# The last output projection of a two-layer backbone: from feature-major tiles to token-major pieces

## The reference

```
for i in range(DEPTH):
    need_ctx = i < DEPTH - 1
    ...
    h_lat = h_lat + g_l * (o_lat @ w_out[i])
    if need_ctx:
        h_ctx = h_ctx + g_c * (o_ctx @ w_out[i])
return h_lat
```

## Time and profile before

| what | value |
|---|---|
| median of 3 runs | 1484.33 us (1481.15, 1484.33, 1485.0) |
| the profiled execution: its time, its span | 1482.72 us, 1480.9 us |
| mean granted TensorE clock (1.0 is 2.4 GHz) | 0.992 |
| PE busy, VectorE busy, ScalarE busy | 97%, 67%, 37% of the span |
| first projection without its first tile, 841.0 to 1002.4 us | 161.4 us |
| norm stage, 1002.4 to 1040.4 us | 38.0 us |
| store of `hT` (L885): issued, landed after; SP's next weight load | 1005.9 us, 9.7 us; 1023.7 us |
| last projection, 1380.4 to 1475.6 us, and what follows it | 95.2 us, 5.3 us |

### The profile page before, as it was taken

The page is one execution under the profiler, slowest core; times in us unless marked ns, Lnnn a source line. Parts: engine busy times, 40 slices in busy tenths (PEclk is TensorE's granted clock), DMA queues, the critical chain, the costliest instruction groups (busy, mean ns, idle before and its releaser), DMA issues.

```text
span 1480.9 us, 18435 instructions
## 1 busy us (share of the span) xinstructions
PE 1434.7 (97%) x7415; PEld 1144.5 (77%) x7415; DVE 986.2 (67%) x1196; ACT 541.1 (37%) x764; POOL 237.3 (16%) x272
## 2 busy tenths in 40 slices
PE   5989999999999999999999899998999899999998
PEld 1336878888887878778888688888888778788998
DVE  3384998889988877786786554547455766555543
ACT  2554222221221433443323411216256455455432
POOL 1000333323332000000002043342000110000000
PEclk9999999999999999999999999999999999999999
DMA  9999555565555554454555766544334432323563
GB/s 344 400 360 347 193 176 169 156 227 156 185 168 150 193 185 135 132 170 175 164 209 203 257 216 230 200 152 132 114 114 143 142 114 90 110 87 113 191 221 129
DMA packets 65172, 272.23 MB, mean 184 GB/s; under 512 B 6784, under 2 KB 17216, under 8 KB 45376
## 3 DMA queue, kind: packets, MB, share of 16 engines
q1 hardware_dynamic: 44912, 193.45, 37.1%
q0 software_dynamic: 20176, 77.61, 16.2%
HBM read 256.36 MB, written 14.68 MB: 183 GB/s over the span
## 4 chain that ended last, share of the span: by engine, by line
PE 90%; DMA 4%; DVE 3%; ACT 1%; issue 1%; SPq 0%; ACTq 0%; POOL 0%; DVEq 0%
PE banks L1036 20%; PE banks L1037 20%; PE banks L1040 20%; DMA ada_ring<-in_ada_first 3%; PE banks L1984 2%; PE banks L1985 2%; PE banks L1990 2%; PE banks L1218 2%; PE banks L2147 2%; PE banks L1205 2%; PE banks L2019 1%; PE banks L1301 1%; PE banks L551 1%; PE banks L2118 1%; PE banks L2134 1%; PE banks L1269 1%
## 5 line engine op out<-in xcount | busy, mean ns | idle before, releaser
L1036 PE MATMUL banks<-xh,wh 128*128 128x512 f32 (+1 forms) x1536 | 538.3, 363 | 0.1
L1037 PE MATMUL banks<-xl,wh 128*128 128x512 f32 (+1 forms) x1536 | 525.3, 355 | 0.0
L998 DVE TENSOR_TENSOR wl<-raw,wh 128x2048 fp32r<-128x2048 f32 (+1 forms) x125 | 283.7, 2270 | 96.4 <-ACT wh L992 96.3
L1036 PEld LDWEIGHTS banks<-xh,wh 128*128 128x128 f32 x1536 | 290.1, 189 | 49.6 <-issue 9.3
L992 ACT ACTIVATE wh<-raw 128x2048 fp32r<-128x2048 f32 (+1 forms) x125 | 236.5, 1892 | 242.1 <-PE banks L1040 171.3
L1037 PEld LDWEIGHTS banks<-xl,wh 128*128 128x128 f32 x1536 | 290.3, 189 | 43.3 <-issue 3.8
L1040 PE MATMUL banks<-xh,wl 128*128 128x512 f32 (+1 forms) x1536 | 311.0, 355 | 0.0
L1040 PEld LDWEIGHTS banks<-xh,wl 128*128 128x128 f32 x1536 | 256.9, 189 | 40.5
L386 DVE SCALAR_TENSOR_TENSOR ada_acc<-ada_w,cond,ada_acc 128x1024 f32<-128x1024 f32 x120 | 160.1, 1334 | 5.1 <-DMA ada_w<-in_ada_rest 2.9
L409 POOL DMA_DIRECT2D ada_w<-in_ada_rest x128 | 69.3, 542 | 556.4 <-DVE ada_acc L398 381.4
L398 DVE SCALAR_TENSOR_TENSOR ada_acc<-ada_w,cond,ada_acc 128x1024 f32<-128x1024 f32 x90 | 125.3, 1392 | 0.0
(11 more groups left out here) (329 smaller groups left out, 1704.7 us busy)
## 6 DMA issues: line engine op xcount, KB each, us to landing
ada_w<-in_ada_rest POOLq DMA_DIRECT2D x128, 512.0 KB, 4.1
raw<-in_ev_tiles SPq DMA_DIRECT2D x52, 1024.0 KB, 6.7
ada_ring<-in_ada_first SPq DMA_DIRECT2D x32, 1024.0 KB, 12.4
raw<-in_out_tiles SPq DMA_DIRECT2D x32, 1024.0 KB, 5.1
raw<-in_od_wide SPq DMA_DIRECT2D x16, 1024.0 KB, 4.9
raw<-in_od_gates SPq DMA_DIRECT2D x16, 1024.0 KB, 4.9
hT<-in_hT POOLq DMA_DIRECT2D x4, 1024.0 KB, 11.9
spectra<-kstage POOLq DMA_DIRECT2D x4, 1024.0 KB, 10.6
```

Source lines behind the costliest of these rows:

```text
L998: nc.vector.tensor_tensor(b.wl[:, t % 2, 0:width], b.raw[:, t % 2, 0:width], b.wh[:, t % 2, 0:width].bitcast(F32), ALU.subtract).then_inc( ...
L1036: nc.tensor.matmul(out, wh[:, k, :], b.xh[:, seg, k, :], start=(k == 0), stop=False)
L1037: nc.tensor.matmul(out, wh[:, k, :], b.xl[:, seg, k, :], start=False, stop=False)
```

## The change

The last projection is written anew (`last_block`) and done token-major: four pieces of 512 output columns, each of four weight tiles (512 rows of `w_out` by 512 columns, 1024 KB as before) for two halves r of 128 tokens. Per weight tile and half there are 12 matmuls of 512 columns, with `xh` or `xl` as the stationary operand. The weight rows are taken in the order in which the attention units end (`WIDE_ROWS`). A piece is finished by VectorE in two steps per half: product times a broadcast row of gates (`grow`), plus the residual in token order (`hrow`). SP stores each half by itself (256 KB).

What that needs is made earlier. The first projection turns each hT tile after the next product (`turn_residual`; the last one in the norm stage), ScalarE copies four tiles at a time (`copy_residual`, after the splits of i = 5, 9, 13 and at the end of the norm stage), SP stores 512 KB four times (`store_residual`), the last time in layer 1. The gate column block is turned in the norm stage by one more transpose, copied, stored as a row of 8 KB and loaded back broadcast to 128 partitions (1024 KB) at slot 32 of layer 1. The store of `hT` and the waits on it go. Semaphores are renamed or shared (`gains_in` is now `spread_in`; `odd_mx` and `odd_rden` are joined to layer 0's), and `out_block` serves the first projection alone; the parts of the diff that do only that are left out.

```diff
-    return {"ev_tiles": tiles(a["ev_w_in"][0]), "out_tiles": np.stack([tiles(w) for w in a["w_out"]]),
+    return {"ev_tiles": tiles(a["ev_w_in"][0]), "out_tiles": tiles(a["w_out"][0]),
+            "out_wide": np.concatenate([wide(a["w_out"][1][:, c:c + 512]) for c in range(0, D, 512)]),
...
+    b.otok_late = put("otok_late", "ADA", 0, [P, 2, 512])
+    b.gate_rows = put("gate_rows", "ADA", 4 * K, [KT, P])
+    b.hrow = [put(f"hrow{c}", "EX", 4 * K * c, [P, 2, 512]) for c in range(2)]
+    b.grow = put("grow", "C", 3 * K, [P, D])
...
     def _(sp):
         for i in (2, 3):
             load_raw(sp, b, s, t + i, *l1_weights(g, i))
-        sp.wait_ge(s.out_added, 2 * KT)
-        sp.dma_start(g.hres_d[:, :, 0:256], b.hT[:, :, 0:256]).then_inc(s.h_out, 16)
-        sp.wait_ge(s.h_out, 16)
...
         last.then_inc(s.norm_spread, 1)
+        turn_residual(nc, pe, b, s, ps, KT - 1)
+        pe.wait_ge(s.ada_stored, ADA_GROUP_STORES + len(ADA_CHUNKS))
+        nc.tensor.transpose(ps[6][0:KT, 0:P], b.ada[:, 1, 0, 32:48], b.ident).then_inc(s.out_turned, 1)
...
+        copy_residual(nc, act, b, s, ps, 3)
+        act.wait_ge(s.out_turned, KT + 1)
+        nc.scalar.activation(b.gate_rows[:], ps[6][0:KT, 0:P], ACT.Copy).then_inc(s.out_copied, 1)
...
+def turn_residual(nc, pe, b, s, ps, j):
+
+    grp = j // 4
+    pe.wait_ge(s.out_added, 2 * (j + 1))
+    if j % 4 == 0 and grp >= 2:
+        pe.wait_ge(s.out_copied, 2 * (grp - 1))
+    for r in range(2):
+        last = nc.tensor.transpose(ps[2 + 2 * (grp % 2) + r][:, P * (j % 4):P * (j % 4) + P],
+                                   b.hT[:, j, P * r:P * r + P], b.ident)
+    last.then_inc(s.out_turned, 1)
+
+
+def copy_residual(nc, act, b, s, ps, grp):
+
+    act.wait_ge(s.out_turned, 4 * (grp + 1))
+    if grp == 2:
+        act.wait_ge(s.h_out, 16)
+    for r in range(2):
+        out = b.otok_late[:, r, :] if grp == 3 else b.otok[:, grp % 2, r, :]
+        nc.scalar.activation(out, ps[2 + 2 * (grp % 2) + r], ACT.Copy).then_inc(s.out_copied, 1)
+
+
+def store_residual(sp, b, s, g, grp):
+
+    sp.wait_ge(s.out_copied, 2 * (grp + 1))
+    sp.dma_start(g.htok_d[:, :, 512 * grp:512 * grp + 512].rearrange("r p n -> p r n"),
+                 b.otok_late[:] if grp == 3 else b.otok[:, grp % 2]).then_inc(s.h_out, 16)
...
+            if i in (7, 11, 15):
+                store_residual(sp, b, s, g, i // 4 - 1)
...
-        if layer == 1:
-            out_store(3)
-            for r in range(2):
-                sp.wait_ge(s.out_tok_out[r], 32)
-
...
-            if layer == 1 and i >= 1:
-                to_tokens(i - 1)
-        if layer == 1:
-            to_tokens(OUT_TILES - 1)
...
+                pe.wait_ge(s.out_added, 2 * (i - 1))
+            product(nc, pe, b, s, t0 + i, ps[i % 2], ready=(s.out_o_high, s.out_o_low) if i == 0 else None)
+            if i >= 1:
+                turn_residual(nc, pe, b, s, ps, i - 1)
...
+            split_high(nc, act, b, s, t0 + i + 1, l1_width(0) if i + 1 == OUT_TILES else D)
+            if i in (5, 9, 13):
+                copy_residual(nc, act, b, s, ps, i // 4 - 1)
...
+WIDE_ROWS = (2, 3, 0, 1)
+OUT_BANKS = ((2, 3), (0, 1))
+
+
+def wide_weights(g, i):
+
+    return g.out_wide[4 * (i // 4) + WIDE_ROWS[i % 4]].rearrange("p (k n) -> p k n", k=4), (4, 512)
+
+
+def last_block(nc, blk, b, s, ps, g, t0):
+
+    added = 2 * KT
+
+    @blk.sync
+    def _(sp):
+        def load_rows(c):
+            if c >= 2:
+                sp.wait_ge(s.out_added, added + 2 * (c - 1))
+            if c == 1:
+                sp.wait_ge(s.odd_pv, 16)
+            sp.dma_start(b.hrow[c % 2][:], g.htok_d[:, :, 512 * c:512 * c + 512].rearrange("r p n -> p r n")).then_inc(
+                s.out_res_in[c % 2], 16)
+
+        def store(c):
+            for r in range(2):
+                sp.wait_ge(s.out_added, added + 2 * c + r + 1)
+                sp.dma_start(g.out[0, P * r:P * r + P, 512 * c:512 * c + 512], b.otok[:, c % 2, r, :]).then_inc(
+                    s.out_tok_out[c % 2], 16)
+
+        load_rows(0)
+        for i in range(2, OUT_TILES):
+            load_raw(sp, b, s, t0 + i, *wide_weights(g, i))
+            if i in (3, 7, 11):
+                load_rows(i // 4 + 1)
+            if i in (6, 10, 14):
+                store(i // 4 - 1)
+        store(3)
+        for c in range(2):
+            sp.wait_ge(s.out_tok_out[c], 64)
+
+    @blk.tensor
+    def _(pe):
+        for i in range(OUT_TILES):
+            c, kk = divmod(i, 4)
+            t = t0 + i
+            wh, wl = chunk_weights(b, t, 512)
+            pe.wait_ge(s.hi_done, t + 1)
+            for r in range(2):
+                if c == 1 and kk == 0:
+                    pe.wait_ge(s.gate_drained, KT)
+                if c >= 2 and kk == 0:
+                    pe.wait_ge(s.out_added, added + 2 * (c - 2) + r + 1)
+                out = ps[OUT_BANKS[c % 2][r]]
+                rows = slice(P * r, P * r + P)
+                for k in range(4):
+                    n = 4 * WIDE_ROWS[kk] + k
+                    if c == 0:
+                        pe.wait_ge(s.odd_o_high, 4 * kk + k + 1)
+                    nc.tensor.matmul(out, b.xh[:, 1, n, rows], wh[:, k, :], start=(kk == 0 and k == 0), stop=False)
+                    if c == 0:
+                        pe.wait_ge(s.odd_o_low, 4 * kk + k + 1)
+                    nc.tensor.matmul(out, b.xl[:, 1, n, rows], wh[:, k, :], start=False, stop=False)
+                pe.wait_ge(s.lo_done, t + 1)
+                for k in range(4):
+                    last = nc.tensor.matmul(out, b.xh[:, 1, 4 * WIDE_ROWS[kk] + k, rows], wl[:, k, :], start=False,
+                                            stop=(kk == 3 and k == 3))
+                if r == 1:
+                    last.then_inc(s.proj_done, 1)
+                elif kk == 3:
+                    last.then_inc(s.out_half, 1)
+
+    @blk.scalar
+    def _(act):
+        for i in range(OUT_TILES - 1):
+            split_high(nc, act, b, s, t0 + i + 1)
+
+    @blk.vector
+    def _(dve):
+        for i in range(OUT_TILES):
+            if i + 1 < OUT_TILES:
+                split_low(nc, dve, b, s, t0 + i + 1)
+            if i % 4 < 3:
+                continue
+            c = i // 4
+            dve.wait_ge(s.spread_in, 32)
+            dve.wait_ge(s.out_res_in[c % 2], 16 * (KT // 2 + c // 2 + 1))
+            if c >= 2:
+                dve.wait_ge(s.out_tok_out[c % 2], 32)
+            for r in range(2):
+                if r:
+                    dve.wait_ge(s.proj_done, t0 + i + 1)
+                else:
+                    dve.wait_ge(s.out_half, c + 1)
+                x = b.otok[:, c % 2, r, :]
+                nc.vector.tensor_tensor(x, ps[OUT_BANKS[c % 2][r]], b.grow[:, 512 * c:512 * c + 512], ALU.mult).then_inc(
+                    s.out_scaled, 1)
+                dve.wait_ge(s.out_scaled, 2 * c + r + 1)
+                nc.vector.tensor_tensor(x, x, b.hrow[c % 2][:, r, :], ALU.add).then_inc(s.out_added, 1)
...
     def _(sp):
         for i in range(4, L1_TILES):
             load_raw(sp, b, s, t0 + i, *l1_weights(g, i))
+            if i == 6:
+                store_residual(sp, b, s, g, 3)
+                sp.wait_ge(s.out_copied, 9)
+                sp.dma_start(g.gate_d[0].rearrange("(k p) -> k p", p=P), b.gate_rows[:]).then_inc(s.h_out, 16)
+            if i == 32:
+                sp.wait_ge(s.h_out, 80)
+                for r in range(2):
+                    sp.wait_ge(s.tok_turned[r], len(ROTATED))
+                sp.dma_start(b.grow[:], g.gate_d.to_broadcast((P, D))).then_inc(s.spread_in, 16)
         for i in range(2):
-            load_raw(sp, b, s, t0 + L1_TILES + i, out_weights(g, 1, i), (KT, P))
+            load_raw(sp, b, s, t0 + L1_TILES + i, *wide_weights(g, i))
...
             if kk == 0:
+                if kind == "kv":
+                    pe.wait_ge(s.out_copied, 9)
...
-        act.wait_ge(s.h_out, 16)
...
+            if turned == 1:
+                act.wait_ge(s.h_out, 80)
...
-        dve.wait_ge(s.h_out, 16)
...
-    g.hres_d = nc.dram_tensor("residual", (P, KT, T), F32, kind="Internal").ap()
+    g.htok_d = nc.dram_tensor("residual", (2, P, D), F32, kind="Internal").ap()
+    g.gate_d = nc.dram_tensor("gate_row", (1, D), F32, kind="Internal").ap()
```

More of the change, by code:

```diff
@@ L1013, in pair_product, with product @@
     return nc.tensor.matmul(out, wh[:, k, :], b.xl[:, :, k, :], start=False, stop=(k == KT - 1))
-def product(nc, pe, b, s, t, bank, first=0, count=2, ready=None, order=range(KT)):
+def product(nc, pe, b, s, t, bank, first=0, count=2, ready=None):
     pe.wait_ge(s.hi_done, t + 1)
@@ L1026, in product @@
         pe.wait_ge(s.lo_done, t + 1)
-        for n, k in enumerate(order):
-            pe.wait_ge(ready[0], n + 1)
-            nc.tensor.matmul(out, wh[:, k, :], b.xh[:, seg, k, :], start=(n == 0), stop=False)
+        for k in range(KT):
+            pe.wait_ge(ready[0], k + 1)
```

(47 more changed lines are left out.)

111 lines of the change are left out of this document (34 added, 77 removed).

## The result

The changed kernel takes **1475.72 us** (median of 4 runs, 1475.0 to 1476.37), the kernel before 1484.2 us beside it (1481.15 to 1485.0). The ratio is 0.9948, 95% interval 0.9931 to 0.9965. The profiled execution took 1475.96 us, of it 1474.2 in the span; that of before 1482.72 and 1480.9.

A forecast was written before the change was run, and what follows sets the result against it. PE's own work was taken to bound the kernel, nine tenths of the chain that ended last. Terms -8.1 + 3.1 - 1.4 = -6.4 us on 1483.4 gave 1477.0 us; own range 1475 to 1479, overall range 1474 to 1481.5.

The forecast's parts named there:

- The last projection: 768 narrow matmuls become 384 of 512 columns and the transposes leave: -8.1 us, 3.2 of it the transposes.
- The rival in which the fixed part isn't saved: Last projection: wide matmuls take 0.240 us, as two narrow ones, so only the transposes' time is saved; 1481.9 us, 4%.
- The pairs: First projection: 14 added pairs of transposes stand between products on a busy PE, 0.22 us each, +3.1 us.
- The rival of 0.45: First projection: each added pair of transposes costs 0.45 us, its weight load being exposed; +3.2 us, 1480.2 us, 5%.
- The norm stage and layer 1: Added transposes, copies and the broadcast load there are hidden by waits and slack: 0 us; 3.5 us cover 1.4 of copies.
- The clock's dip at the norm's start: PE at 1.2 GHz for 4.9 us costs 2.4 us; rivals: no dip 1474.6 us, twice as long 1479.4, 6% each.
- The end: From the last product to the kernel's end 3.9 us instead of 5.3: -1.4 us, at least -0.6.
- The weight chain: Last projection: a buffer's round of 9.5 us per two tiles fits PE's 10.9, 1.4 us to spare: 0 us.
- the second rival: Last projection: weight loads are late at the piece borders only, costing 4.2 us in the middle; 1481.2 us, 13%.
- splits that wait for loads: Last projection, sign of a wrong prediction: ScalarE's split waits for a load, where it should still wait for PE.
- The first rival: Last projection: weight loading becomes the bound once loads take over 6.3 us on average; at 8.1 the end is 1491, 5%.
- The base: Time before the change, 1483.4 us, the middle between the profiled execution's 1482.7 and the runs' median of 1484.3.

## Why the prediction came out as it did

The kernel took 1475.7 us, 1.3 below the 1477.0 forecast and inside its own range of 1475 to 1479. By its steps:

- **The last projection**, forecast -8.1, measured -8.06. That the fixed part is saved, the step on which it rested, is shown by the narrow products in the new roles: 5.0 of the 8.06 come back. The rest, 3.0 us, is the transposes that left (3.2 by the prediction's rows). The rival in which the fixed part isn't saved is refuted. The 2.5 ns that the prediction took from the Trainium skill, page "TensorE: Matmul & The Clock Gate", section "Back-to-back issue gap", are given there for an isolated matmul, and the section says that in a stream of weight loads and matmuls the distance comes out otherwise; such a stream is what this kernel has. The prediction left that out. The runs have 13 ns with 4-byte operands and over 11 with 2-byte ones.
- **The pairs**, forecast +3.1, measured +3.50. The mechanism was right, and the size of 0.22 too low by 0.03: the first products behind the pair lose that too. Without the pairs it is gone to the last 0.01 us. The rival of 0.45 is refuted.
- **The norm stage and layer 1**, forecast 0, measured -0.06. The cover ahead of kv is real: 3.7 us more work on ScalarE still fit, 7.4 didn't. It was worked out too small, though: the 4.9 us from the split's end at 1035.5 to kv at 1040.4 are the cover, and the 3.5 called so are what the copies leave of it. The clock's dip at the norm's start neither vanished nor grew. Its price of 2.4 us was put a little high: without the dip the norm's products take 28.40 us, 2.2 less than the 30.56 and 30.61 with it, since the 13 ns are missing at the lower level.
- **The end**, forecast -1.4, measured -1.3: issue and landing took 2.6 us instead of 2.4.
- **The weight chain**, forecast 0, measured 0. Its margin was smaller than worked out, for a load landed after 5.1 us instead of 4.9: 0.33 + 5.1 + 1.92 + 2.29 = 9.64 of 10.88 us. The lateness that the second rival put at the piece borders does occur, twice and by half a us at most, but a single late load has slack, and PE didn't idle. The prediction named splits that wait for loads as a sign of being wrong; three do, at no cost. The first rival's mechanism is real too: with landings of 8.1 us from the fifth tile on it takes 8.7 us and all of the gain, where the prediction had 13.9 for such landings throughout. At 7.0 us, which it names as the end of the gain, eight rounds of 11.5 us would lose 5.3 of its 6.4 us, not all.
- **The base.** The terms sum to -5.9 instead of -6.4. The time came out lower than forecast nonetheless, and that is luck, since the base of 1483.4 was high: all 46 runs of the kernel before have a median of 1482.6, from 1478.8 to 1487.1, and the changed kernel's 10 runs one of 1476.0, a difference of 6.6. The 0.7 us between this and the 5.9 of the stretches are within the spread and not traced further. Some 4 us of this spread arise ahead of the change: in the profiles here the second tile's third products begin between 844.05 and 848.06 us, though no kernel here changes the work up to there.

## What to carry to other kernels

Where PE is busy throughout, price a matmul by its distance to the next at two widths; the part that doesn't shrink with the columns (13 ns here, at full clock) is saved by halving the number, whatever the roles of the operands. Transposes moved between such products cost their full distance and a little per interruption; placed where PE waits anyway they cost nothing here, and with 16 of them there the clock also stayed up in two of three executions. Before PE is made faster in a stage fed by loads, add up one round of a buffer (issue, landing, splits) and see how much longer a landing it bears: here 1.2 us, and 3 us more turned the gain into a loss.

## What was not expected of the hardware

A wait of PE of 3.3 us ahead of kv cost about 5.2 us, since the granted clock fell to its lower level behind it. At that level the wide products stood 0.427 us apart, twice the 0.213 that their columns cost at full clock and without the fixed 13 ns that they have there. Operands of two bytes, whose weight loads took 96 ns instead of 188, took under 2 ns off those 13. With 16 transposes in the norm's waits, 8 in each, the granted clock stayed at 1.00 through the norm's start in both executions of the kernel with half of the pairs there; in the one with unused transposes there it fell all the same, so such work didn't keep it up every time.
